# Adaptive vectors of a Conformer and MLA block: all their sums on TensorE, with turns of the identity between them

## What is computed

```python
c_act = jax.nn.silu(c)
shift, scale, gate = jnp.split(c_act @ w_ada[l] + b_ada[l], 3, axis=-1)
h = rms_norm(x, norm_w[l]) * (1.0 + scale[:, None, :]) + shift[:, None, :]
proj = h @ w_in[l]
```

## Time and profile before

| | us |
|---|---|
| median of 3 runs | 2557.09 |
| lowest and highest run | 2556.83, 2558.12 |
| the profiled execution, its own time | 2556.22 |
| its span, first to last instruction | 2554.4 |
| VectorE busy, share of the span | 1716.9 (67%) |
| ScalarE busy, share of the span | 882.3 (35%) |
| GpSimd busy, share of the span | 682.4 (27%) |

### The profile page before, as it was taken

The page is one execution under the profiler, slowest core; times in us unless marked ns, Lnnn a source line. Parts: engine busy times, 40 slices in busy tenths (PEclk is TensorE's granted clock), DMA queues, the critical chain, the costliest instruction groups (busy, mean ns, idle before and its releaser), DMA issues. The chain is left out here.

```text
span 2554.4 us, 30658 instructions
## 1 busy us (share of the span) xinstructions
PE 2519.1 (99%) x11930; PEld 2091.1 (82%) x11930; DVE 1716.9 (67%) x2166; ACT 882.3 (35%) x1749; POOL 682.4 (27%) x615
## 2 busy tenths in 40 slices
PE   6999999999999999999999999999999999999998
PEld 5788888888888888888888888888888788888887
DVE  6778697989889898857467777677677521223343
ACT  5452111111111111234466566556566511111221
POOL 1222111111111111143144344244244310423322
PEclk9999999999999999999999999999999999999999
DMA  8133321313213121289824224224224273757532
GB/s 315 43 102 100 92 58 59 92 50 92 58 59 89 52 84 46 62 269 315 295 102 136 83 73 140 79 73 141 79 71 139 62 237 132 247 190 237 190 129 83
DMA packets 192155, 316.47 MB, mean 124 GB/s; under 512 B 14248, under 2 KB 106476, under 8 KB 181387
## 3 DMA queue, kind: packets, MB, share of 16 engines
q1 hardware_dynamic: 181984, 288.93, 34.6%
q0 software_dynamic: 5120, 16.78, 2.0%
q10 hardware_dynamic: 4907, 8.81, 0.9%
HBM read 207.52 MB, written 106.95 MB: 123 GB/s over the span
## 5 line engine op out<-in xcount | busy, mean ns | idle before, releaser
L53 PE MATMUL ps_proj<-h_hi,w_hi 128*128 128x512 f32 x1664 | 654.0, 393 | 4.7 <-DVE h_lo L987 4.7
L54 PE MATMUL ps_proj<-h_lo,w_hi 128*128 128x512 f32 x1664 | 648.3, 390 | 0.0
L55 PE MATMUL ps_proj<-h_hi,w_lo 128*128 128x512 f32 x1664 | 648.2, 390 | 0.0
L1096 DVE SCALAR_TENSOR_TENSOR acc<-u,front_only,acc 128x2048 f32<-128x2048 f32 x240 | 629.0, 2621 | 8.5
L867 POOL TENSOR_TENSOR w_lo<-raw,w_hi 128x1024 fp32r<-128x1024 f32 x50 | 170.5, 3411 | 789.2 <-ACT w_hi L573 789.2
L53 PEld LDWEIGHTS ps_proj<-h_hi,w_hi 128*128 128x128 f32 x1664 | 312.9, 188 | 70.8 <-DVE h_lo L987 5.5
L55 PEld LDWEIGHTS ps_proj<-h_hi,w_lo 128*128 128x128 f32 x1664 | 312.8, 188 | 65.5
L54 PEld LDWEIGHTS ps_proj<-h_lo,w_hi 128*128 128x128 f32 x1664 | 313.0, 188 | 64.8 <-issue 1.4
L2118 POOL TENSOR_SCALAR prob<-prob,rinv 128x512 f32<-128x512 f32 (+2 forms) x320 | 199.4, 639 | 339.8 <-DVE rinv L1998 337.1
L2063 DVE TENSOR_TENSOR pt_lo<-ps_t,pt_hi 128x512 fp32r<-128x512 f32 (+1 forms) x320 | 193.4, 607 | 66.3 <-ACT pt_hi L1976 62.8
L750 ACT ACTIVATE lat<-ps_proj 128x512 f32<-128x512 f32 x120 | 72.0, 600 | 466.1 <-PE ps_proj L55 417.1
(11 more groups left out here) (287 smaller groups left out, 4076.0 us busy)
## 6 DMA issues: line engine op xcount, KB each, us to landing
qlat<-qlat_dram SPq DMA_DIRECT2D x32, 1024.0 KB, 7.6
raw<-in_w_in_dram SPq DMA_DIRECT2D x50, 512.0 KB, 6.4
under_h<-in_w_ada_dram SPq DMA_DIRECT2D x8, 1024.0 KB, 14.2
ga_dram<-lat SPq DMA_DIRECT2D x8, 1024.0 KB, 5.0
gb_dram<-lat SPq DMA_DIRECT2D x8, 1024.0 KB, 5.2
agate_dram<-lat SPq DMA_DIRECT2D x8, 1024.0 KB, 5.0
conv_dram<-acc SPq DMA_DIRECT2D x8, 1024.0 KB, 3.9
v_dram<-v_st SPq DMA_DIRECT2D x4, 2048.0 KB, 8.4
```

Of the source, the lines that this page charges most:

```text
L53: pe.matmul(out, wh, xh, start=first, stop=False)
L54: pe.matmul(out, wh, xl, start=False, stop=False)
L55: return pe.matmul(out, wl, xh, start=False, stop=last)
L1096: dve.scalar_tensor_tensor(acc[:], u[:, n:n + S], tap(n), acc[:], ALU.mult, ALU.add).then_inc(conv_tap if n < TAPS - 1 else conv_done, 1)
```

## The change

VectorE's sums go, and TensorE takes all 8 row blocks of each w_ada block with silu(c), each half summed in PSUM in its own columns, as soon as that half is there. Behind each half it makes 6 turns of the identity into a bank that nobody reads (`WARM`). The turns of pieces 0 to 3 of x come after block 1 instead of after block 0. The last half of w_ada comes in two transfers with a semaphore each, and its second part is summed in columns of its own. Shift and gain are added up from these three places.

The high part of the first weight pair is made in two halves, behind ScalarE's pieces 1 and 2 instead of ahead of piece 0; VectorE makes the first low part behind piece 0 instead of ahead of it; TensorE starts on piece 0 with the products that need no low part. The squares of chunk 1 are taken two by two behind pieces 4 and 5 instead of one by one behind pieces 2 to 5. The others keep their places.

The diff, without the declarations:

```diff
     AHEAD = 4
+    WARM = 6
     BEHIND = 2
+    SQUARES = {4: (4, 5), 5: (6, 7)}
+    SQUARES.update({i - QB + BEHIND: (i,) for i in range(2 * QB, TT)})
     N_PIECE = NC_ * KT
     X_BANKS = [[1, 5, 2, 6], [3, 7, 2, 6], [0, 4, 3, 7], [1, 5, 0, 4]]
     MEAN_BANK = [4, 5, 6, 7, 6, 7, 2, 3]
...
+        ada_last = sem("ada_last")
         sums_done = sem("sums_done")
         root_done = sem("root_done")
...
 
+        def ada_parts(j, kh):
+            if (j, kh) == (ADA_J - 1, 1):
+                return [(range(0, KH // 2), ada_in[j][kh]), (range(KH // 2, KH), ada_last)]
+            return [(range(0, KH), ada_in[j][kh])]
...
                 for kh in range(2):
-                    sp.dma_start(wada_at[j][kh], w_ada[:, kh * KH:(kh + 1) * KH, chunk(j)]).then_inc(ada_in[j][kh], 16)
+                    for of, to in ada_parts(j, kh):
+                        sp.dma_start(wada_at[j][kh][:, of.start:of.stop, :],
+                                     w_ada[:, kh * KH + of.start:kh * KH + of.stop, chunk(j)]).then_inc(to, 16)
 
             def first_pair():
...
 
-                if tile < 2:
-                    act.wait_ge(raw_in[0], 16)
-                    act.activation(weights(tile)[0][:], k.raw_pair[:, :, tile * P:(tile + 1) * P], ACT.Copy).then_inc(
-                        hi_made, 1)
-                    return
                 act.wait_ge(raw_in[tile % 2], raw_need(tile))
...
                 act.activation(weights(tile)[0][:], raw[tile % 2][:], ACT.Copy).then_inc(hi_made, 1)
+
+            def first_pair_hi(half):
+                act.wait_ge(raw_in[0], 16)
+                ts = slice(half * KH, (half + 1) * KH)
+                for tile in range(2):
+                    act.activation(weights(tile)[0][:, ts, :], k.raw_pair[:, ts, tile * P:(tile + 1) * P],
+                                   ACT.Copy).then_inc(hi_made, 1)
 
             def square_x(i):
...
                 act.activation(x_at[i], x_at[i], ACT.Identity, scale=ss[:, i:i + 1]).then_inc(x_scaled, 1)
-            split_hi(0)
-            split_hi(1)
             act.wait_ge(ada_vec, 6)
             for n in range(N_PIECE):
                 turn_out(n)
-                if 0 <= n - BEHIND < TT - QB:
-                    square_x(QB + n - BEHIND)
+                if n in (1, 2):
+                    first_pair_hi(n - 1)
+                for i in SQUARES.get(n, ()):
+                    square_x(i)
                 c, t = divmod(n - KT, KT)
                 if c >= 0 and t == AHEAD - 1:
...
             def split_lo(tile):
-                pool.wait_ge(hi_made, tile + 1)
+                pool.wait_ge(hi_made, tile + 3)
                 if tile == KEY:
                     w = weights(tile)[0]
...
 
-            dve.wait_ge(params_sb, 1)
-            dve.tensor_scalar(cact_part[:], k.cact[:, KT - 1:KT], 1.0 / D, None, ALU.mult).then_inc(ada_step, 1)
-            for j in range(ADA_J):
-                if j >= 2:
-                    dve.wait_ge(ada_mm, 2 * (j - 1))
-                for n in range(KT - 1):
-                    kh, t = divmod(n, KH)
-                    if t == 0:
-                        dve.wait_ge(ada_in[j][kh], 16)
-                    if (j, n) == (0, KT - 2):
-                        invert_x(0)
-                    a, w = ada_acc[j % 2], wada_at[j][kh][:, t, :]
-                    if n == 0:
-                        ins = dve.tensor_scalar(a, w, k.cact[:, n:n + 1], None, ALU.mult)
-                    else:
-                        dve.wait_ge(ada_step, (KT - 1) * j + n + 1)
-                        ins = dve.scalar_tensor_tensor(a, w, k.cact[:, n:n + 1], a, ALU.mult, ALU.add)
-                    ins.then_inc(ada_step, 1)
-
+            invert_x(0)
             dve.wait_ge(params_sb, 3)
-            dve.wait_ge(ada_mm, 2 * ADA_J - 1)
-            dve.scalar_tensor_tensor(shift[:], ps_tail[:, 0:KT], float(D), k.prm_t[:, R_BADA:R_BADA + KT],
-                                     ALU.mult, ALU.add).then_inc(ada_vec, 1)
-            dve.scalar_tensor_tensor(gain[:], ps_tail[:, KT:2 * KT], float(D),
-                                     k.prm_t[:, R_BADA + KT:R_BADA + 2 * KT], ALU.mult, ALU.add).then_inc(ada_vec, 1)
+            dve.wait_ge(ada_mm, 2 * ADA_J)
+            dve.tensor_tensor(shift[:], ps_ada[0][:, 0:KT], k.prm_t[:, R_BADA:R_BADA + KT], ALU.add).then_inc(ada_vec, 1)
+            dve.scalar_tensor_tensor(gain[:], ps_ada[0][:, KT:2 * KT], 1.0, k.prm_t[:, R_BADA + KT:R_BADA + 2 * KT],
+                                     ALU.add, ALU.add).then_inc(ada_vec, 1)
+            dve.wait_ge(ada_vec, 1)
+            dve.tensor_tensor(shift[:], ps_ada[1][:, 0:KT], shift[:], ALU.add).then_inc(ada_vec, 1)
             dve.wait_ge(ada_vec, 2)
-            dve.tensor_scalar_add(gain[:], gain[:], 1.0).then_inc(ada_vec, 1)
-            dve.wait_ge(ada_mm, 2 * ADA_J)
-            dve.scalar_tensor_tensor(shift[:], ps_ada[:, 0:KT], float(D), shift[:], ALU.mult, ALU.add).then_inc(ada_vec, 1)
-            dve.wait_ge(ada_vec, 3)
-            dve.scalar_tensor_tensor(gain[:], ps_ada[:, KT:2 * KT], float(D), gain[:], ALU.mult, ALU.add).then_inc(ada_vec, 1)
+            dve.tensor_tensor(gain[:], ps_ada[1][:, KT:2 * KT], gain[:], ALU.add).then_inc(ada_vec, 1)
+            dve.wait_ge(ada_mm, 2 * ADA_J + 1)
+            dve.wait_ge(ada_vec, 4)
+            dve.tensor_tensor(gain[:, KT - QB:KT], ps_tail[:, 2 * KT - QB:2 * KT], gain[:, KT - QB:KT],
+                              ALU.add).then_inc(ada_vec, 1)
             dve.wait_ge(ada_vec, 5)
             dve.tensor_tensor(gain[:], gain[:], k.prm_t[:, R_NORM:R_NORM + KT], ALU.mult).then_inc(ada_vec, 1)
+
             def first_pair_lo(ts):
                 for tile in range(2):
-                    dve.wait_ge(hi_made, tile + 1)
+                    dve.wait_ge(hi_made, 2 * (ts.start // KH) + tile + 1)
                     ins = dve.tensor_tensor(weights(tile)[1][:, ts, :], k.raw_pair[:, ts, tile * P:(tile + 1) * P],
                                             weights(tile)[0][:, ts, :].bitcast(F32), ALU.subtract)
                     if ts.stop == KT:
                         ins.then_inc(lo_made, 1)
+                return ins
 
             for n in range(N_PIECE):
                 g, t = divmod(n, KT)
                 hi, lo = (a[g][:, t, :] for a in (k.h_hi, k.h_lo))
-                if n < KT and n % 2 == 0:
+                if 0 < n < KT and n % 2 == 0:
                     first_pair_lo(slice(n, n + 2))
                 dve.wait_ge(full_done, n + 1)
                 dve.tensor_copy(hi, full[n % 2]).then_inc(h_hi_done, 1)
                 dve.wait_ge(h_hi_done, n + 1)
-                dve.tensor_tensor(lo, full[n % 2], hi.bitcast(F32), ALU.subtract).then_inc(h_lo_done, 1)
+                ins = dve.tensor_tensor(lo, full[n % 2], hi.bitcast(F32), ALU.subtract)
+                if n == 0:
+                    ins = first_pair_lo(slice(0, 2))
+                ins.then_inc(h_lo_done, 1)
                 if (n - BEHIND) % QB == QB - 1 and 0 <= n - BEHIND < TT - QB:
                     invert_x((n - BEHIND) // QB + 1)
...
             def ada_products(j):
-                pe.wait_ge(ada_in[j][1], 16)
-                pe.wait_ge(ada_step, 1)
-                for m in range(TC // P):
-                    mm = pe.matmul(ps_tail[:, j * QB + m:j * QB + m + 1], wada_at[j][1][:, KH - 1, m * P:(m + 1) * P],
-                                   cact_part[:], start=True, stop=True)
-                mm.then_inc(ada_mm, 1)
-                pe.wait_ge(ada_step, (KT - 1) * (j + 1) + 1)
-                for m in range(TC // P):
-                    mm = pe.matmul(ps_ada[:, j * QB + m:j * QB + m + 1], ada_acc[j % 2][:, m * P:(m + 1) * P],
-                                   k.mean_mat[:, 0:1], start=True, stop=True)
-                mm.then_inc(ada_mm, 1)
+                for kh in range(2):
+                    for n, (of, landed) in enumerate(ada_parts(j, kh)):
+                        to = ps_tail if n else ps_ada[kh]
+                        pe.wait_ge(landed, 16)
+                        for m in range(TC // P):
+                            for t in of:
+                                mm = pe.matmul(to[:, j * QB + m:j * QB + m + 1], wada_at[j][kh][:, t, m * P:(m + 1) * P],
+                                               k.cact[:, kh * KH + t:kh * KH + t + 1], start=t == of[0], stop=t == of[-1])
+                        mm.then_inc(ada_mm, 1)
+                        if n == 0:
+                            for _ in range(WARM):
+                                pe.transpose(ps[:, 0, 0:P], k.ident[:], k.ident[:])
 
             def turn_x(n):
...
             ada_products(0)
+            ada_products(1)
             for n in range(AHEAD):
                 turn_x(n)
-            ada_products(1)
             ada_products(2)
             ada_products(3)
             for n in range(N_PIECE):
                 g, t = divmod(n, KT)
-                pe.wait_ge(h_lo_done, n + 1)
-                for tile in range(2):
```

(19 more changed lines are left out.)

## The result

The changed kernel takes 2599.16 us (median of 4 runs, 2598.89 to 2599.91) against 2556.99 for the kernel before, a ratio of 1.0164 with a 95% interval of 1.0147 to 1.0182. It is slower, inside the range on record and 4.8 us under the number forecast. Its profiled execution took 2599.05 us.

The account below looks back on a forecast made before the run. TensorE was taken as the bound, busy 2519.1 of 2554.4 us. 2556.2 (profiled execution) + 44.8 (sums) + 2.4 (behind T) = 2603.4, said as 2604 since the median is 0.9 higher; range 2570 to 2610.

Parts of the forecast that it names:

- TensorE becomes the bound of the setup: Setup sums: a half costs TensorE 8.1 us and arrives every 2.75 us, no load wait behind the first; +44.8 us.
- 0.213 us a record: Setup sums: each one-column product takes two records of 0.213 us; 256 records take 54.5 us.
- The clock stays at the lower level: TensorE in the setup: half clock throughout, despite the idle turns; chance 0.67, range of its own 2598 to 2610 us.
- now and then full clock: Rival, setup sums: 22 turns in a row behind block 1 may raise the clock; 2587 or 2599; 0.13 for under 2597.
- Full clock from early on: Rival, setup sums: the steady stream raises the clock some 4.3 us in; time 2573 to 2574 us; chance 0.14.
- The last half in two transfers costs nothing: Last w_ada half: one more issue on the queue, worth nothing and costing nothing, as TensorE comes some 40 us late.
- Behind T, +2.4 us: After the last sum: chunk 1 starts about T + 19.5 instead of T + 17.1, +2.4 us; bounds +0.4 and +5.
- T: End of TensorE's last sum for shift and gain in the setup: forecast at 81.4 us, against 36.6 before.
- T + 12.8: ScalarE's root of chunk 1's squares: forecast 12.8 us after T, with 1.2 us for two waits.
- Nothing gained from x landing early: Behind the sums: x landing early gains nothing, since its squares stand behind T in both kernels.
- T + 10.4: ScalarE's root of chunk 1's squares in the kernel before: 10.4 us after T.

Follow-up runs that it names:

- The swapped form: Changed kernel with the sums' operands swapped (a column of c is the weight, 512 columns of w_ada move), no idle turns, last half in one transfer: 2569.61 us.
- the run of the sums alone that had no rise: Changed kernel with the part behind the sums undone, 2596.65 us; its fourth run, with a mean granted clock of 1.000, took 2599.75 us.
- the one with half of the sums: Changed kernel with every second row block of w_ada left out of the sums, all still loaded: 2569.43 us.

## Why the prediction was right, and where it was off

- *TensorE becomes the bound of the setup.* Shown: no wait on a load from 13.46 to 77.89, and half of the records take the time with them (27.3 us due, 29.7 measured by the medians, with a longer rise of the clock).
- *0.213 us a record.* Shown by 128 records in 27.5 us in the run without idle turns. In the changed kernel a half with its turns took 8.0 us, not 8.1; over eight halves that is 0.7 us of the difference.
- *The clock stays at the lower level.* Right for most of the stretch, wrong as a whole. The rival "now and then full clock" named the very place, 22 turns in a row behind block 1, and gave it too small a chance; it took 3.2 us off (2.4 in the half from 48.27, 0.8 in the turns ahead of it), in all four runs by their mean granted clocks. The step that failed is the reading of the earlier trace rows: I took 16 turns without a rise, in one execution, as evidence that turns don't raise the clock. The run with 22 turns shows that they do. Here the range held and the rival's mechanism came with it: without the rise the time would have been 2602.4, 1.6 us from the forecast. The Trainium skill, "TensorE: Matmul & The Clock Gate", Part 4, says that full clock does not engage for transposes; the runs here differ from it (granted clock 0.85 and 0.93 in the stretches behind 22 turns), and they decide.
- *Full clock from early on*, the rival that goes with Part 1 of the same page of the Trainium skill, by which sustained activity releases the throttle, did not come either: TensorE was busy without a gap from 13.5 on and its starts kept the distance of the lower level to 47.3; after the rise it fell at some 51 within one-column products. The swapped form, with 512 columns moving, kept full clock.
- *The last half in two transfers costs nothing.* Off by 0.8 us, for the idle turns that it puts ahead of the last sums: the prediction weighed the issue and the load and not where the idle turns would stand.
- *Behind T, +2.4 us.* Root at T + 12.8 and chunk 1 at T + 19.5, both as forecast; put in alone, the part costs 2.3 us at chunk 1 and 1.7 by the medians; undone, it gives 3.2 at chunk 1 and 2.5 by the medians. I had expected one wait ahead of chunk 1; there are two (1.52 on VectorE's low part, 1.11 on GpSimd), so TensorE was not through with chunk 0 at T + 16.7.
- *Nothing gained from x landing early.* Off by up to 0.8 us at chunk 1. It doesn't show in the + 2.4, because the sum for T + 12.8 had no wait on x in it while the T + 10.4 of the kernel before has one: the new order costs 3.2 and the early x gives 0.8 back.

The account of the profiled execution: 2603.4 forecast, + 0.4 (first half landed at 13.46), - 0.7 (pace), - 3.2 (clock), - 0.8 (the span grew by 42.9 us, chunk 1 moved by 43.7; I can name only small waits in the attention, 1.7 us on VectorE's low parts before and 1.1 after, and the rest of the kernel varies by 2 us between the traces anyway) gives 2599.1, and 2599.05 was measured. The terms under a microsecond may hide each other, so the agreement to 0.1 us is luck. The 3.2 us are shown, by this trace and by the run of the sums alone that had no rise.

## What to carry to other kernels

A product with one column is not a cheap product: here it took 0.43 us at the lower clock and 0.22 at the upper. Its two records start as far apart as turns that move 128 columns, so the moving column doesn't set the price; that the load of 128 x 128 weights does is my reading, and no run changes the weights alone. Before work goes to another engine, its time for one arriving piece has to be held against the distance at which pieces arrive; here it was 8.0 against 2.75 us, and at full clock, with 38 instructions at 0.11, it would still have been 4.2. Where a filler is meant to keep the clock up, take it out and count both, and look that it doesn't stand ahead of the instruction that everything waits for.

## What the runs showed of the hardware that I had not expected

- Turns between one-column products raised the clock, without any product of 512 columns; 16 in a row did it in some executions and not in others, and 22 in 18 of 20 runs, by their mean granted clocks. One-column products alone did not, in 27.5 us. The profiled execution of the kernel before kept 0.213 us behind 16 turns; the same instructions in the run with the part behind the sums took 1.03 us for 8 records at 26.48, which is full clock, and the granted clock averages 0.73 over 25.4 to 34.0. Among 13 runs of the kernel before, beside these, four read a mean of 0.996 or 0.997, as that execution does. It changes nothing in the time there, but it does in the kernels whose setup TensorE bounds: the run without idle turns spread over 5.3 us, the one with half of the sums over 8.1 us.
- TensorE, busy without a gap, lost full clock in one-column products (granted 1.00 at 49.3 to 50.3, 0.50 from 51.3); in the swapped form, with 512 columns moving, it kept it to the end of the sums.
- The granted clock reads 1.00 from the start of a trace up to the first fall, though the distances of starts show the lower level (0.213 us from 13 to 47, 0.11 at 48). A mean such as 0.993 for the changed kernel so leaves out half of its slow time: the 34 us from 13.5 to 47.3, as long as the stretch at 0.50 from 51 to 85.
